# The last expert of each mixture of experts: its gated rows split and loaded ahead, its result in two column halves

## The chip, the cores and the metric
The kernel runs on one core of one Trainium2 chip. The metric is device time in microseconds (us), the median of three runs. One execution is also taken by the hardware profiler, and the trace is of that one. Engines are named as in the profile: PE is TensorE (matmul), PEld its weight loads, DVE is VectorE, ACT is ScalarE, POOL is GpSimd, SP is SyncE.

## The reference
Two layers of a diffusion backbone over 512 tokens of width 1024: layer 0 mixes with retention and differential attention, layer 1 with a pooling mixer. Each layer ends in a mixture of 16 experts with hidden width 512, of which each token uses two:

```
for e in range(N_EXPERTS):
    hid = silu(flat @ w_gate[e]) * (flat @ w_up[e])
    out = out + combine[:, e:e + 1] * (hid @ w_down[e])
x = x + g2 * out
```

The output is the RMS norm of x after both layers. Everything is fp32.

## The kernel before
The program is a row of stages, each a block with one instruction stream per engine, closed by a barrier of all engines. The stages that matter here are the two mixtures (`moe(0)` ahead of the pooling layer, `moe(1)` ahead of the final norm). After each of them a stage follows that does nothing unless an expert has more than 128 tokens, and then a stage whose first work is on POOL: eight indirect DMAs (L2165) that gather each token's two result rows from `y_dram` in HBM. Those rows are written by the mixture, so the mixture's stage ends only when its last store has landed.

A mixture works on one expert at a time, on at most 128 of its tokens. For fp32 accuracy each matmul operand is split into a high part (fp32r) and a low part (the rest), and each product is three matmuls: high by high, high rows by low weights, low rows by high weights. ACT makes the high parts (`high`, L1725, for the weights; L1732 for the rows; `hid_high`, L1741, for the gated rows), and DVE the low parts (`low`, L1879; L1886; `hid_low`, L1896). The weights of an expert come in six halves p = 0 to 5: gate (0, 1), up (2, 3) and down (4, 5), loaded by SP into a ring (L475). The parts of a half live in one of four buffers, `buf(u, p)`.

Step e holds the down product of expert e and the gate and up products of expert e + 1. On PE its order is: gate product of e + 1 (24 matmuls of 512 columns, L1978), four transposes of the gated rows of e (L2006) into PSUM bank 4, eight transposes for the rows of expert e + 2 (L1961), up product of e + 1 (24 matmuls), and the down product of e (`down`, L1993, 12 matmuls for each of p = 4 and 5) into banks 6 and 7. On DVE: low part of half 0, low part of the rows, the gating of e + 1 (`hidden`, L1892), low parts of halves 1 to 3, the result of expert e - 1 out of banks 6 and 7 times the layer's gate (`rows_out`, L1903), `hid_low`, and the low parts of halves 4 and 5. On ACT: the high parts in step with this, `hid_high`, the silu for e + 1, the store of e - 1 (L1745, a DMA on ACT's own queue) and the high part of half 5. All of this is in program order on each engine, with semaphores that count: `s_used` for halves that PE is done with, `s_hi` and `s_lo` for parts, `s_ht2`, `s_hhi` and `s_hlo` for the gated rows' transposes, high and low parts, `s_y` for results and `s_yst` for stores.

Step 15, the last, has no expert after it. It is only: transposes of the gated rows of 15, `hid_high`, `hid_low`, the parts of its two down halves, its 24 down matmuls, the eviction of all 1024 columns and one store of 512 KB.

Of the kernel before, what the change touches and what calls it, by code (L numbers as in the profile page):

```python
# [31 lines left out]
P = 128  # L32
# [7 lines left out]
HALF = 512  # L40
# [70 lines left out]
def build_program(nc, a, out):  # L111
    ctx = ExitStack()
    with ctx, nc.allow_non_contiguous_dma(reason="short rows of small tables"):
# [71 lines left out]
        def stage_sb(name, shape, dt=F32):  # L185
            return mem["stack"].enter_context(nc.sbuf_tensor(f"{name}{mem['stages']}", shape, dt))
# [1362 lines left out]
        def moe(l):  # L1549
# [17 lines left out]
            xT_lo = stage_sb("xT_lo", [P, KD, P], F32R)  # L1567
            hT_hi = stage_sb("hT_hi", [P, KE, P], F32R)
            hT_lo = stage_sb("hT_lo", [P, KE, P], F32R)

            mark = stage_sb("mark", [1, 1])

# [53 lines left out]
            def last_step(e):  # L1626
                return isinstance(e, int) and e == LAST

            def buf(u, p):

                return (2 * u + p) % 4
# [4 lines left out]
            def pos_count(e, p):  # L1636

                return count(6, p - 4 if last_step(e) else p, e)
# [11 lines left out]
            with nc.Block() as block:  # L1650
# [65 lines left out]
                @block.scalar  # L1716
                def _(act):
                    def high(e, u, p):

                        act.wait_ge(half_load[raw(e, p)], loaded(e, p))  # L1720
                        if isinstance(e, int) and e == 0 and p < 4:
                            act.wait_ge(s_used, (1, 2, 3, 6)[p])
                        elif not (isinstance(e, int) and e == -1):
                            act.wait_ge(s_used, pos_count(e, p) - 4)
                        nc.scalar.copy(w_hi[:, buf(u, p), :], half(raw(e, p))).then_inc(s_hi, 3 if isinstance(e, int) and (e, p) == (-1, 3) else 1)  # L1725

                    def rows_high(n, b, up_used):

                        act.wait_ge(s_gt, n + 1)
                        if up_used is not None:  # L1730
                            act.wait_ge(s_used, up_used)
                        nc.scalar.copy(xT_hi[:, b].rearrange("p k t -> p (k t)"),  # L1732
                                       bank[:, 0:2, :].rearrange("p b c -> p (b c)")).then_inc(s_xhi, 1)

                    def silu(n, gate_used):
                        act.wait_ge(s_used, gate_used)
                        nc.scalar.activation(act_g, bank[:, 2, :], ACT.Silu).then_inc(s_silu, 1)

                    def hid_high(n):
                        act.wait_ge(s_ht2, n + 1)  # L1740
                        nc.scalar.copy(hT_hi[:].rearrange("p k t -> p (k t)"), bank[:, 4, :]).then_inc(s_hhi, 1)  # L1741

                    def store(e, u):
                        act.wait_ge(s_y, e + 1)
                        act.dma_start(y_dram[bass.ds(e * P, P), :], y_sb[:, u, :]).then_inc(s_yst[u], 16)  # L1745

                    def step(e, u):
                        if isinstance(e, int) and e == 0:
                            high(0, 0, 0)
                            silu(0, pos_count(-1, 1))  # L1750
                            rows_high(1, 1, None)
                            for p in (1, 2, 3):
                                high(0, 0, p)
                        elif not last_step(e):
                            high(e, u, 0)
                            rows_high(e + 1, 1 - u, pos_count(e, 3) - 12)
                            for p in (1, 2, 3):
                                high(e, u, p)
                        high(e, u, 4)
                        hid_high(e)  # L1760
                        if not last_step(e):
                            act.wait_ge(s_hid, e + 1)
                            silu(e + 1, pos_count(e, 1))
                        if not (isinstance(e, int) and e == 0):
                            store(e - 1, 1 - u)
                        high(e, u, 5)

                    for p in range(4):
                        high(-1, 0, p)
                    rows_high(0, 0, None)  # L1770
                    step(0, 0)
                    with act.Fori(0, (NE - 4) // 2) as i:
                        for v in range(2):
                            step(2 * i + 1 + v, 1 - v)
                    for e in range(NE - 3, NE):
                        step(e, e % 2)
                    store(NE - 1, 1)
                    for u in range(2):
                        act.wait_ge(s_yst[u], 16 * (NE // 2 + 1))

                @block.vector
                def _(dve):
# [93 lines left out]
                    def low(e, u, p):  # L1876

                        dve.wait_ge(s_hi, pos_count(e, p))
                        V.tensor_tensor(w_lo[:, buf(u, p), :], half(raw(e, p)), w_hi[:, buf(u, p), :].bitcast(F32),  # L1879
                                        ALU.subtract).then_inc(s_lo, 3 if isinstance(e, int) and (e, p) == (-1, 3) else 1)  # L1880

                    def rows_low(n, b, up_used):
                        dve.wait_ge(s_xhi, n + 1)
                        if up_used is not None:
                            dve.wait_ge(s_used, up_used)
                        V.tensor_tensor(xT_lo[:].rearrange("p k t -> p (k t)"), bank[:, 0:2, :].rearrange("p b c -> p (b c)"),  # L1886
                                        xT_hi[:, b].rearrange("p k t -> p (k t)").bitcast(F32), ALU.subtract).then_inc(s_xlo, 1)
# [3 lines left out]
                        dve.wait_ge(s_silu, n + 1)  # L1891
                        V.tensor_tensor(hid, act_g, bank[:, 3, :], ALU.mult).then_inc(s_hid, 1)  # L1892

                    def hid_low(n):
                        dve.wait_ge(s_hhi, n + 1)
                        V.tensor_tensor(hT_lo[:].rearrange("p k t -> p (k t)"), bank[:, 4, :],  # L1896
                                        hT_hi[:].rearrange("p k t -> p (k t)").bitcast(F32), ALU.subtract).then_inc(s_hlo, 1)

                    def rows_out(n, u, down_used, stored):

# [3 lines left out]
                                        ALU.mult).then_inc(s_y, 1)  # L1904

                    def step(e, u, stored):
                        if not last_step(e):
                            low(e, u, 0)
                            rows_low(e + 1, 1 - u, pos_count(e, 3) - 6)
                        hidden(e, 6 * (e + 1) - 2)  # L1910
                        if not last_step(e):
                            low(e, u, 1)
                            low(e, u, 2)
                            low(e, u, 3)
                        if stored is not None:
                            rows_out(e - 1, 1 - u, 6 * (e + 1), stored)
                        hid_low(e)
                        low(e, u, 4)
                        low(e, u, 5)
# [8 lines left out]
                    with dve.Fori(0, (NE - 4) // 2) as i:  # L1928
                        for v in range(2):
                            step(2 * i + 1 + v, 1 - v, 16 * i + 16)  # L1930
                    for e in range(NE - 3, NE):
                        step(e, e % 2, 16 * ((e - 1) // 2) + 16)
                    rows_out(NE - 1, 1, pos_count(LAST, 5), 16 * (LAST // 2) + 16)

                @block.tensor
                def _(pe):
# [57 lines left out]
                                                     start=(kk == 0 and i == 0), stop=(kk == KE - 1 and i == 2))  # L1994
                        last.then_inc(s_used, 1)

                    def step(e, u, gathered):

                        if not last_step(e):
                            pe.wait_ge(s_xlo, e + 2)  # L2000
                            pe.wait_ge(s_silu, e + 1)
                            product(2, e, u, 0, 1 - u)
                            product(2, e, u, 1, 1 - u)
                        pe.wait_ge(s_hid, e + 1)
                        for k in range(KE):
                            last = pe.transpose(bank[:, 4, k * P:(k + 1) * P], hid[:, k * P:(k + 1) * P], ident[:])  # L2006
                        last.then_inc(s_ht2, 1)
                        if gathered is not None:
                            rows_T(u, gathered)
                        if not last_step(e):  # L2010
                            product(3, e, u, 2, 1 - u)
                            product(3, e, u, 3, 1 - u)
                        pe.wait_ge(s_hlo, e + 1)
                        if not (isinstance(e, int) and e == 0):
                            pe.wait_ge(s_y, e)
                        down(e, u, 4)
                        down(e, u, 5)

                    keep_busy(16)
                    rows_T(0, 16)  # L2020
# [8 lines left out]
                    with pe.Fori(0, (NE - 4) // 2) as i:  # L2029
                        for v in range(2):  # L2030
                            step(2 * i + 1 + v, 1 - v, 16 * i + 16 * (2 + v))
                    for e in range(NE - 3, NE):
                        step(e, e % 2, 16 * ((e + 2) // 2 + 1) if e + 2 < NE else None)

            stage_over()

# [363 lines left out]
```

## Time and profile before

| | us |
|---|---|
| median of three runs (1180.56 to 1181.78) | 1181.64 |
| the profiled execution | 1180.51 |
| its span in the profile | 1178.7 |
| PE busy | 1044.6 (89%) |
| DVE busy | 928.9 (79%) |
| ACT busy | 608.0 (52%) |
| POOL busy | 162.1 (14%) |

Times in the rows are in us from the start of the span. "Idle before" a group is how long its engine did nothing ahead of it, and "<-" names what ended that. A matmul row's length is that of the whole pass through the array, so neighbouring matmuls overlap: what one costs in a stream is the distance between two starts. PEclk is the share of full speed that was granted to TensorE's clock. The expert products of the first mixture run from 474 to 764, and those of the second end at 1147.

### The profile page before, as it was taken

What the parts mean: (1) busy time and instruction counts of PE and PEld (TensorE: products, weight loads), DVE (VectorE), ACT (ScalarE), POOL (GpSimd) and SP (SyncE); (2) the same over time, 40 slices, a digit from 0 to 9 for tenths busy, and PEclk for the clock granted to TensorE, in tenths of its full rate; (3) what the DMA queues carried; (4) which work ended last, traced back from release to release, by engine and by line L of the source; (5) the groups of instructions that cost most, each with busy time, mean ns of one, the idle gap of its engine ahead of it and who ended that gap; (6) DMA issues with size and microseconds to landing.
All of it is one profiled execution on the core that took longest, in us unless ns stands there. A gap on an engine that the chain in (4) does not pass through costs nothing. (4 is left out here: it accounts for less than half of the span.)

```text
span 1178.7 us, 13896 instructions
## 1 busy us (share of the span) xinstructions
PE 1044.6 (89%) x4832; PEld 795.7 (68%) x4832; DVE 928.9 (79%) x1041; ACT 608.0 (52%) x614; POOL 162.1 (14%) x172
## 2 busy tenths in 40 slices
PE   6789999998898987999999999738799999999970
PEld 1476767766565445788888888637578888888850
DVE  4578888877993336799999999555759999999955
ACT  1534222213664113677777777333367777777831
POOL 0100200000100002522212210041341000000006
PEclk9899999999999997999999999959799999999995
DMA  9715878676014003999999999576399999999936
GB/s 372 263 64 206 284 283 302 223 281 232 7 66 134 36 29 135 301 412 414 413 414 414 413 414 413 206 250 274 98 269 401 414 413 414 414 414 414 413 131 232
DMA packets 145693, 332.44 MB, mean 282 GB/s; under 512 B 14064, under 2 KB 16056, under 8 KB 145520
## 3 DMA queue, kind: packets, MB, share of 16 engines
q1 hardware_dynamic: 125768, 277.99, 62.3%
q10 hardware_dynamic: 12392, 28.68, 6.5%
q0 software_dynamic: 7488, 25.19, 5.7%
q8 instruction: 26, 0.43, 0.1%
q14 instruction: 19, 0.16, 0.0%
HBM read 308.72 MB, written 23.15 MB: 282 GB/s over the span
## 5 line engine op out<-in xcount | busy, mean ns | idle before, releaser
L1879 DVE TENSOR_TENSOR w_lo<-ring,w_hi 128x2048 fp32r<-128x2048 f32 x192 | 432.2, 2287 | 26.1 <-ACT w_hi L1725 22.5
L1725 ACT CAST w_hi<-ring 128x2048 fp32r<-128x2048 f32 x192 | 365.4, 1915 | 135.2 <-DMA ring<-in_moe_w_up 59.8
L1978 PE MATMUL bank<-w_hi,xT_hi 128*128 128x512 f32 x512 | 203.4, 397 | 6.7 <-DVE xT_lo L1886 5.2
L1978 PE MATMUL bank<-w_hi,xT_lo 128*128 128x512 f32 x512 | 199.9, 390 | 0.0
L1978 PE MATMUL bank<-w_lo,xT_hi 128*128 128x512 f32 x512 | 199.4, 389 | 0.0
L1399 PE MATMUL bank<-ring_last_parts,arena_parts 128*128 128x512 f32 (+1 forms) x320 | 117.1, 397 | 5.4 <-DVE ring_parts L1016 2.7
L1978 PEld LDWEIGHTS bank<-w_hi,xT_hi 128*128 128x128 f32 x512 | 96.1, 188 | 28.4 <-DVE xT_lo L1886 6.9
L1978 PEld LDWEIGHTS bank<-w_hi,xT_lo 128*128 128x128 f32 x512 | 96.1, 188 | 20.8
L1074 DVE SCALAR_TENSOR_TENSOR gate_b<-ring,silu_c,gate_b 128x512 f32<-128x512 f32 x140 | 105.9, 757 | 4.5
L1978 PEld LDWEIGHTS bank<-w_lo,xT_hi 128*128 128x128 f32 x512 | 96.3, 188 | 19.0
L1993 PE MATMUL bank<-w_hi,hT_hi 128*128 128x512 f32 x256 | 101.0, 394 | 7.5 <-DVE w_lo L1879 7.5
L1993 PE MATMUL bank<-w_lo,hT_hi 128*128 128x512 f32 x256 | 101.1, 395 | 0.0
L1993 PE MATMUL bank<-w_hi,hT_lo 128*128 128x512 f32 x256 | 100.9, 394 | 0.0
L1399 PE MATMUL bank<-ring_parts,arena_parts 128*128 128x512 f32 (+1 forms) x256 | 99.9, 390 | 0.0
L1399 PEld LDWEIGHTS bank<-ring_last_parts,arena_parts 128*128 128x128 f32 x320 | 60.1, 191 | 31.5 <-issue 13.2
L1399 PE MATMUL bank<-ring_last_parts,x_parts 128*128 128x512 f32 x192 | 76.8, 400 | 0.0
L1682 POOL DMA_INDIRECT shared<-xh_scratch,shared x32 | 62.6, 1957 | 60.7 <-DVE shared L1870 52.6
L1993 PEld LDWEIGHTS bank<-w_hi,hT_hi 128*128 128x128 f32 x256 | 48.9, 191 | 18.5 <-issue 8.3
L767 ACT CAST ring_last_parts<-ring 128x1024 fp32r<-128x1024 f32 x24 | 25.2, 1051 | 67.2 <-PE bank L1399 61.5
L1993 PEld LDWEIGHTS bank<-w_hi,hT_lo 128*128 128x128 f32 x256 | 48.9, 191 | 10.3
L1993 PEld LDWEIGHTS bank<-w_lo,hT_hi 128*128 128x128 f32 x256 | 48.6, 190 | 10.2
L1903 DVE TENSOR_TENSOR shared<-bank,gate_b 128x1024 f32<-128x1024 f32 x32 | 39.0, 1219 | 19.8 <-PE bank L1993 19.8
(254 smaller groups left out, 1397.5 us busy)
## 6 DMA issues: line engine op xcount, KB each, us to landing
ring<-in_moe_w_gate SPq DMA_DIRECT2D x64, 1024.0 KB
ring<-in_moe_w_up SPq DMA_DIRECT2D x64, 1024.0 KB, 13.4
ring<-in_moe_w_down SPq DMA_DIRECT2D x64, 1024.0 KB, 11.6
ring<-in_ada_w SPq DMA_DIRECT2D x21, 2048.0 KB, 8.6
y_scratch<-shared ACTq DMA_DIRECT2D x32, 512.0 KB, 6.1
ring<-in_w_in ACTq DMA_DIRECT2D x21, 512.0 KB, 3.8
shared<-in_ada_w SPq DMA_DIRECT2D x2, 2048.0 KB, 16.0
x_res<-in_x SPq DMA_DIRECT2D x8, 512.0 KB, 12.4
```

The source lines that it names most:

```text
L767: nc.scalar.copy(w_high(n), w_raw(n)).then_inc(m_whi, 1)
L1074: ins = nc.vector.scalar_tensor_tensor(ada_acc[:, i % 2, :], w[:, k, :], silu_c[:, 0, k:k + 1], onto, ALU.mult, ALU.add)
L1399: last = pe.matmul(acc(u)[:, c0:c1], hs[h_], ws[w_], start=(kk == 0 and i == 0), stop=(kk == KD - 1 and i == 2))
L1682: pool.indirect_dma_start(out=xg[:, u, :], out_offset=None, in_=xh_dram, in_offset=bass.IndirectOffsetOnAxis(ap=idx[:, c:c + 1], axis=0)). ...
L1725: nc.scalar.copy(w_hi[:, buf(u, p), :], half(raw(e, p))).then_inc(s_hi, 3 if isinstance(e, int) and (e, p) == (-1, 3) else 1)
L1879: V.tensor_tensor(w_lo[:, buf(u, p), :], half(raw(e, p)), w_hi[:, buf(u, p), :].bitcast(F32), ALU.subtract).then_inc(s_lo, 3 if isinstance ...
L1903: V.tensor_tensor(y_sb[:, u, :], bank[:, 6:8, :].rearrange("p b c -> p (b c)"), gate2_b[:], ALU.mult).then_inc(s_y, 1)
L1978: last = pe.matmul(bank[:, b, :], xs[:, kk, :], ws[:, k, :], start=(kk == 0 and i == 0), stop=(kk == KD - 1 and i == 2))
L1993: last = pe.matmul(bank[:, 6 + hf, :], xs[:, kk, :], ws[:, k, at], start=(kk == 0 and i == 0), stop=(kk == KE - 1 and i == 2))
```

## The change
In the step of expert 14, the four transposes of expert 15's gated rows are put between the two halves of expert 14's down product. The high and low parts of those gated rows go into new places, `hT_last_hi` and `hT_last_lo`, which are the two halves of a buffer for expert rows that is free by then. On ACT both high parts of expert 15's down halves now come ahead of `hid_high`, and the store of expert 14 comes after it. On DVE the order after step 14 is: gating of 15, low part of half 4, `hid_low`, low part of half 5, `rows_out` of expert 14, and then the result of 15 in two halves of 512 columns. On PE `down_last` takes the place of `down` for expert 15: it writes banks 0 and 1 and not 6 and 7, does all 12 matmuls of one column half (both p) and then all 12 of the other, and each is stored by a DMA of its own. The branches `last_step` in the helpers go.

```diff
+            hT_last_hi, hT_last_lo = xT_hi[:, 0, 0:KE, :], xT_hi[:, 0, KE:KD, :]
...
 act:
-                    for e in range(NE - 3, NE):
+                    for e in range(NE - 3, LAST):
                         step(e, e % 2)
-                    store(NE - 1, 1)
+                    high(LAST, 1, 4)
+                    high(LAST, 1, 5)
+                    hid_high(LAST, hT_last_hi)
+                    store(LAST - 1, 0)
+                    for hf in range(2):
+                        act.wait_ge(s_y, LAST + 1 + hf)
+                        cols_ = slice(hf * HALF, (hf + 1) * HALF)
+                        act.dma_start(y_dram[LAST * P:NE * P, cols_], y_sb[:, 1, cols_]).then_inc(s_yst[1], 16)
                     for u in range(2):
-                        act.wait_ge(s_yst[u], 16 * (NE // 2 + 1))
+                        act.wait_ge(s_yst[u], 16 * (NE // 2 + 1 + u))
...
 dve:
-                    for e in range(NE - 3, NE):
+                    for e in range(NE - 3, LAST):
                         step(e, e % 2, 16 * ((e - 1) // 2) + 16)
-                    rows_out(NE - 1, 1, pos_count(LAST, 5), 16 * (LAST // 2) + 16)
+                    hidden(LAST, 6 * NE - 2)
+                    low(LAST, 1, 4)
+                    hid_low(LAST, hT_last_hi, hT_last_lo)
+                    low(LAST, 1, 5)
+                    rows_out(LAST - 1, 0, 6 * NE, 16 * ((LAST - 1) // 2) + 16)
+                    dve.wait_ge(s_yst[1], 16 * (LAST // 2) + 16)
+                    for hf in range(2):
+                        dve.wait_ge(s_used, pos_count(LAST, 4 + hf))
+                        cols_ = slice(hf * HALF, (hf + 1) * HALF)
+                        V.tensor_tensor(y_sb[:, 1, cols_], bank[:, hf, :], gate2_b[:, cols_], ALU.mult).then_inc(s_y, 1)
...
 pe, in step(e, u, gathered):
                         down(e, u, 4)
+                        if isinstance(e, int) and e == LAST - 1:
+                            hid_T(LAST)
                         down(e, u, 5)
+                    def down_last():
+                        pe.wait_ge(s_hlo, NE)
+                        for hf in range(2):
+                            at = slice(hf * HALF, (hf + 1) * HALF)
+                            for p in (4, 5):
+                                parts(LAST, p)
...
+                                for k in range(KE // 2):
+                                    kk = (p % 2) * (KE // 2) + k
+                                    for i, (xs, ws) in enumerate(((hT_last_hi, hi), (hT_last_hi, lo), (hT_last_lo, hi))):
+                                        last = pe.matmul(bank[:, hf, :], xs[:, kk, :], ws[:, k, at],
+                                                         start=(kk == 0 and i == 0), stop=(kk == KE - 1 and i == 2))
+                            last.then_inc(s_used, 1)
```

## Rows read from the trace of the kernel before

**Rows 1.** The page: busy time, and granted clock in 40 slices.
```profile
PE 1044.6 (89%) x4832; PEld 795.7 (68%) x4832; DVE 928.9 (79%) x1041; ACT 608.0 (52%) x614; POOL 162.1 (14%) x172
PEclk9899999999999997999999999959799999999995
```
**Rows 2.** Waits from 1120 to 1178: engine line <- releaser: total us, times, longest.
```profile
DVE shared L1903 <- PE bank L1993: 9.9, 2, 5.3
PE bank L1993 <- DVE w_lo L1879: 3.8, 1, 3.8
```
**Rows 3.** Timeline of PE, second mixture's end: start, length, engine, line, names.
```profile
1122.36 0.60 PE L2006 MATMUL bank<-ident,shared 128*128 128x128 f32 x4
...
1125.57 0.39 PE L1978 MATMUL bank<-w_hi,xT_hi 128*128 128x512 f32 x1
...
1128.29 0.39 PE L1993 MATMUL bank<-w_hi,hT_hi 128*128 128x512 f32 x1
...
1131.01 0.39 PE L1993 MATMUL bank<-w_hi,hT_hi 128*128 128x512 f32 x1
...
1133.73 0.60 PE L2006 MATMUL bank<-ident,shared 128*128 128x128 f32 x4
1138.10 0.47 PE L1993 MATMUL bank<-w_hi,hT_hi 128*128 128x512 f32 x1 [3.77 <-DVE w_lo L1879]
...
1139.54 0.63 PE L1993 MATMUL bank<-w_hi,hT_lo 128*128 128x512 f32 x1
1139.97 0.63 PE L1993 MATMUL bank<-w_hi,hT_hi 128*128 128x512 f32 x1
...
1145.00 0.39 PE L1993 MATMUL bank<-w_hi,hT_lo 128*128 128x512 f32 x1
```
**Rows 4.** Timeline of DVE, the same stretch.
```profile
1123.61 0.69 DVE L1896 TENSOR_TENSOR hT_lo<-bank,hT_hi 128x512 fp32r<-128x512 f32 x1 [0.66 <-ACT hT_hi L1741]
...
1128.62 0.68 DVE L1892 TENSOR_TENSOR shared<-shared,bank 128x512 f32<-128x512 f32 x1
1133.93 1.23 DVE L1903 TENSOR_TENSOR shared<-bank,gate_b 128x1024 f32<-128x1024 f32 x1 [4.63 <-PE bank L1993]
...
1135.67 4.48 DVE L1879 TENSOR_TENSOR w_lo<-ring,w_hi 128x2048 fp32r<-128x2048 f32 x2
...
1145.43 1.23 DVE L1903 TENSOR_TENSOR shared<-bank,gate_b 128x1024 f32<-128x1024 f32 x1 [5.28 <-PE bank L1993]
```
**Rows 5.** Timeline of ACT, the same stretch.
```profile
1122.99 0.59 ACT L1741 CAST hT_hi<-bank 128x512 fp32r<-128x512 f32 x1 [1.07 <-PE bank L2006]
...
1123.97 3.77 ACT L1725 CAST w_hi<-ring 128x2048 fp32r<-128x2048 f32 x2
1134.36 0.59 ACT L1741 CAST hT_hi<-bank 128x512 fp32r<-128x512 f32 x1 [6.63 <-PE bank L2006]
...
1146.68 0.34 ACTq L1745 DMA_DIRECT2D y_scratch<-shared  x1
```
**Rows 6.** DMA from 1146 to 1153: GB/s in 40 slices of 0.175 us; issues.
```profile
GB/s 0 0 0 0 0 0 0 0 164 421 421 421 421 374 445 328 0 0 0 0 0 0 0 0 0 0 0 0 0 0 0 0 0 0 0 0 0 0 70 140
...
y_scratch<-shared ACTq DMA_DIRECT2D x1, 512.0 KB, 2.6
```
**Rows 7.** Stretches: length, PE, PEld, DVE, ACT, POOL, clock, DMA share, GB/s.
```profile
1128.00:1128.50 0.50, 0.50 (x3) 0.40 (x3) 0.50 (x1) 0.00 (x0) 0.00 (x0) 1.00 0.04 16
1128.50:1129.00 0.50, 0.50 (x4) 0.41 (x3) 0.50 (x2) 0.00 (x0) 0.00 (x0) 1.00 0.00 0
1138.10:1145.40 7.30, 7.29 (x24) 5.54 (x24) 2.05 (x1) 0.00 (x0) 0.00 (x0) 0.77 0.01 2
```
**Rows 8.** Timelines of PE, DVE, POOL and SP, first mixture's end.
```profile
752.10 0.58 SPq L1676 DMA_DIRECT2D mod<-k_band_sum  x1
...
756.55 0.58 PE L1993 MATMUL bank<-w_hi,hT_hi 128*128 128x512 f32 x1 [3.77 <-DVE w_lo L1879]
...
763.89 1.23 DVE L1903 TENSOR_TENSOR shared<-bank,gate_b 128x1024 f32<-128x1024 f32 x1 [5.29 <-PE bank L1993]
...
771.66 0.94 POOL L2165 DMA_INDIRECT arena<-y_scratch,row_of  x1 [78.93 <-issue]
```
**Rows 9.** Timeline of POOL after the second mixture.
```profile
1153.02 0.94 POOL L2165 DMA_INDIRECT shared<-y_scratch,row_of  x1 [80.77 <-issue]
```

More of the change, by code:

```diff
@@ L1737, in silu, with hid_high @@
                         nc.scalar.activation(act_g, bank[:, 2, :], ACT.Silu).then_inc(s_silu, 1)
-                    def hid_high(n):
+                    def hid_high(n, into=hT_hi[:]):
                         act.wait_ge(s_ht2, n + 1)
-                        nc.scalar.copy(hT_hi[:].rearrange("p k t -> p (k t)"), bank[:, 4, :]).then_inc(s_hhi, 1)
+                        nc.scalar.copy(into.rearrange("p k t -> p (k t)"), bank[:, 4, :]).then_inc(s_hhi, 1)
                     def store(e, u):
@@ L1753, in step @@
                                 high(0, 0, p)
-                        elif not last_step(e):
+                        else:
                             high(e, u, 0)
@@ L1760, in step @@
                         hid_high(e)
-                        if not last_step(e):
-                            act.wait_ge(s_hid, e + 1)
-                            silu(e + 1, pos_count(e, 1))
+                        act.wait_ge(s_hid, e + 1)
+                        silu(e + 1, pos_count(e, 1))
                         if not (isinstance(e, int) and e == 0):
@@ L1892, in hidden, with hid_low @@
                         V.tensor_tensor(hid, act_g, bank[:, 3, :], ALU.mult).then_inc(s_hid, 1)
-                    def hid_low(n):
+                    def hid_low(n, hi=hT_hi[:], into=hT_lo[:]):
                         dve.wait_ge(s_hhi, n + 1)
-                        V.tensor_tensor(hT_lo[:].rearrange("p k t -> p (k t)"), bank[:, 4, :],
-                                        hT_hi[:].rearrange("p k t -> p (k t)").bitcast(F32), ALU.subtract).then_inc(s_hlo, 1)
+                        V.tensor_tensor(into.rearrange("p k t -> p (k t)"), bank[:, 4, :],
+                                        hi.rearrange("p k t -> p (k t)").bitcast(F32), ALU.subtract).then_inc(s_hlo, 1)
                     def rows_out(n, u, down_used, stored):
@@ L1906, in step @@
                     def step(e, u, stored):
-                        if not last_step(e):
-                            low(e, u, 0)
-                            rows_low(e + 1, 1 - u, pos_count(e, 3) - 6)
+                        low(e, u, 0)
+                        rows_low(e + 1, 1 - u, pos_count(e, 3) - 6)
                         hidden(e, 6 * (e + 1) - 2)
[L1911 to L1914, printed above, removed]
+                        low(e, u, 1)
+                        low(e, u, 2)
+                        low(e, u, 3)
                         if stored is not None:
@@ L1995, in down, with hid_T @@
                         last.then_inc(s_used, 1)
[L1997 to L2003, printed above, removed]
+                    def hid_T(e):
                         pe.wait_ge(s_hid, e + 1)
@@ L2007, in step @@
                         last.then_inc(s_ht2, 1)
+                    def step(e, u, gathered):
+                        pe.wait_ge(s_xlo, e + 2)
+                        pe.wait_ge(s_silu, e + 1)
+                        product(2, e, u, 0, 1 - u)
+                        product(2, e, u, 1, 1 - u)
+                        hid_T(e)
                         if gathered is not None:
                             rows_T(u, gathered)
-                        if not last_step(e):
-                            product(3, e, u, 2, 1 - u)
-                            product(3, e, u, 3, 1 - u)
+                        product(3, e, u, 2, 1 - u)
+                        product(3, e, u, 3, 1 - u)
                         pe.wait_ge(s_hlo, e + 1)
@@ L2016, in step @@
                         down(e, u, 4)
+                        if isinstance(e, int) and e == LAST - 1:
+                            hid_T(LAST)
                         down(e, u, 5)
+                    def down_last():
[4 more added lines that the diff above has]
+                                parts(LAST, p)
+                                hi = w_hi[:, buf(1, p), :].rearrange("p (k c) -> p k c", c=D)
+                                lo = w_lo[:, buf(1, p), :].rearrange("p (k c) -> p k c", c=D)
+                                for k in range(KE // 2):
[4 more added lines that the diff above has]
+                            last.then_inc(s_used, 1)
                     keep_busy(16)
@@ L2031, in _ @@
                             step(2 * i + 1 + v, 1 - v, 16 * i + 16 * (2 + v))
-                    for e in range(NE - 3, NE):
+                    for e in range(NE - 3, LAST):
                         step(e, e % 2, 16 * ((e + 2) // 2 + 1) if e + 2 < NE else None)
+                    down_last()
             stage_over()
```

## The prediction
> **What bounds the kernel now.** The page comes first. PE is busy 89% of the span and its clock is nearly full in almost every slice [rows 1], so inside the mixtures' steady steps PE sets the pace, and the change leaves those steps alone. The chain of waits reaches back only to the barrier behind the second mixture, so for the mixture's end I go to the waits of the last 60 us: two entries stand out, DVE waiting for PE's down products and PE waiting 3.8 us for a low part [rows 2]. The timelines place them. The up product of expert 15 ends and the down product of 14 runs from 1128.29 to 1133.73 without a hole. Then come the four transposes, and PE does nothing until the down product of 15 starts at 1138.10 [rows 3]. This end is a single file: transposes, high part on ACT at 1134.36 [rows 5], low part on DVE, the low part of half 4 from 1135.67 [rows 4], 24 matmuls, an eviction of 1.23 us, a store issued at 1146.68 [rows 5], its landing, and the barriers before POOL's first gather at 1153.02 [rows 9]. DVE, which makes the part that PE waits for, had itself waited 4.63 us before that for PE [rows 4]. The first mixture has the same end, about 381.5 us earlier: PE starts at 756.55 behind the same hole of 3.77 us, and the last eviction starts at 763.89 [rows 8]. Nothing follows either mixture that could have started without its last store, so what the file loses in length the kernel loses in time, twice.
>
> **The change part by part** (times of the second mixture).
>
> *Transposes moved.* The first half of the down product of 14 ends, by starts, at 1131.01 (12 matmuls in 2.72 us, 0.2267 each) [rows 3]. The transposes need the gating of 15, which runs from 1128.62 to 1129.30 [rows 4], so PE finds it done 1.7 us before. The cost of four transposes within a stream is read at 1122.36: from there to the matmul at 1125.57, which is the thirteenth after them, 3.21 us pass where 12 matmuls take 2.72 [rows 3]. So they cost 0.49 us, and the second half of the down product of 14 ends at 1131.01 + 3.21 = 1134.22.
>
> *What stands behind on ACT.* After step 14 ACT now makes both high parts of 15. The row of two casts from 1123.97 to 1127.74 already holds half 5 of expert 14 and half 4 of 15 [rows 5]; nothing moves there. The cast of half 5 of 15 was behind `hid_high` and ran at 1135.6. It needs its buffer, which PE frees with the last up matmul, about 1128.5, and its weights. The stretches show the DMA traffic of the load end before 1128.5 [rows 7]. So it runs 1128.5 to 1130.4, and ACT is free 1.2 us before `hid_high`, which follows the transposes by 0.63 us as at 1122.99 [rows 3, 5]: 1131.64.
>
> *What stands behind on DVE.* The low part of half 4 follows the gating, 1129.2 to 1131.5 (2.29 us; two take 4.48 [rows 4]). `hid_low` follows `hid_high` by 0.62, as 1123.61 follows 1122.99 [rows 4, 5]: 1132.26. The low part of half 5 begins 0.61 later, 1132.87, and ends at 1135.16. Then `rows_out` of 14 from about 1135.1 to 1136.3, whose banks are complete since 1134.4. Its store is issued at 1136.3, a microsecond later than now, and lands long before the end.
>
> *The down product of 15.* PE waits for `hid_low` (done at 1132.95) and half 4 (1131.5), so it begins at once at 1134.22 and not at 1138.10: **3.88 us** earlier. Because the column half is now the outer loop, half 5 is needed at the seventh matmul and not at the thirteenth: 1134.22 + 6 x 0.2267 = 1135.58. With the 0.14 us that PE took after the low part of half 4 ended at 1137.96 [rows 3, 4], half 5 is there at 1135.30. The cover is 0.28 us: thin, and worth its excess if it fails.
>
> *The clock.* Now the clock falls about a microsecond after PE takes up work behind its 3.77 us of rest: starts are 0.43 us apart at 1139.54, the granted clock of the stretch is 0.77 [rows 3, 7], which is a part at 1.2 and a part at 2.4 GHz. The last matmul starts 6.90 us after the first; at full clock it is 23 x 0.2267 = 5.21. If the hole goes, so should the fall: **1.69 us**. Bounds: nothing if the clock falls anyway, 1.69 if it doesn't. I take all of it, because the step's earlier transposes at 1122.36 sit in a stream whose pitch stays 0.23 [rows 3].
>
> *The eviction.* The last matmul starts at 1134.22 + 5.21 = 1139.43. The new banks leave PE no wait for `rows_out` of 14. The first column half is complete at about 1137.1 and evicted beside PE's second half. DVE took up the last result 0.43 us after the last start (1145.00, 1145.43), so the second half begins at 1139.86. A gating of 512 columns out of PSUM takes 0.68 us [rows 4], against 1.23: **0.55 us**. The issue follows at 1140.55 instead of 1146.68. So far 3.88 + 1.69 + 0.55 = 6.12 (rounded starts make it 6.13).
>
> *The store.* 512 KB takes 2.6 us from issue to landing, of which data flows for 8 slices of 0.175 us, 1.4 us, at some 420 GB/s [rows 6]. The last one is now 256 KB with pieces of 2 KB: 0.7 us less at that rate, nothing less if small pieces or the wait for the write eat it. The store of the first half goes out at 1137.8 and is through by then. I take **0.6 us**, nearer to the transfer's share. The Trainium skill (DMA: Bandwidth & Descriptors, section Anatomy of one DMA) gives an estimate of 2.0 us plus the bytes at 436 GB/s, which would be 3.2 us for the old store and 2.6 for the new. The row has 2.6 for the old one, so the fixed part is smaller here than the page's. If its 2.6 for the new one held all the same, this term would be nothing and the kernel 1.2 us longer than I say.
>
> *Behind it.* From the eviction's start to POOL's first gather are 7.77 us in the first mixture and 7.59 in the second [rows 4, 8, 9]; the barriers in that are unchanged. In the first mixture SP also loads tables for the next stage; its last issue is at 752.10 [rows 8], and the last store there is now issued at 1140.55 - 381.5 = 759.0.
>
> **Sum.** 6.1 + 0.6 = 6.7 us for each mixture, 13.4 for both. The profiled execution took 1180.51 (span 1178.7 and 1.8 around it): 1167.1. The median of the runs lies 1.1 above the profiled one: **1168.2**.
>
> **The rivals.**
> *A wait inside the new file (late half 5).* The cover at the seventh matmul is 0.28 us, and the load of half 5 lands only shortly before its cast. For it: the second mixture's loads run close to their use (the DMA is still busy at 1128 [rows 7]). Against it: ACT has 1.2 us to spare. If the cast or `hid_low` comes 1 to 2 us late, PE stands that long in each mixture: 2 to 4 us in all, 1171.
> *The clock falls anyway,* with some matmuls of the last expert slow. The price is the 1.69 us kept, twice: 1171.6. Against it is the stream around 1122.36.
> *The gain is hidden at the stage's end.* If another engine or SP's tables held the barrier, one mixture would give little: 1168.2 + 6.7 = 1174.9. The tables' rows speak against it, and for the second mixture I see nothing that runs so late.
> *Slower.* The transposes now stand in front of 12 matmuls of expert 14 as well as of the 24 of 15. If the clock fell there and stayed down until the end, 36 matmuls would start 0.43 and not 0.227 apart, 36 x 0.20 = 7.2 us more than in the sum, against its gain of 6.7. That is 0.5 us worse than now in each mixture, 1182.6, and more if the fall begins in the first half of that product too (12 x 0.20 = 2.4 us a mixture: 1187.4). It decides from the 34th slow matmul, 6.7 by 0.20. The transposes at 1122.36 caused no such fall, and now it ends by itself after some 8 slow starts (1.69 by 0.20).
>
> **How the numbers follow.** The forecast has 0.76, with an own range of 1166.0 to 1169.6; the late half 0.10; the clock 0.06; the hidden end 0.05; slower 0.03. The lower end, 1166.0, is the forecast less the 1.2 us by which the three runs spread and 0.5 us in each mixture, 0.1 from the store and 0.4 from releases that I took from single rows. The upper end of its own range has the store saving nothing (1.2) and 0.2; the full range also takes in the late half and the clock: 1166.0 to 1172.0. About 0.2% (2.4 us) is what a measurement can tell from no change: faster 0.96, same 0.02, slower 0.02.
>
> **What would show it.** In the profile after: the four transposes at 1131 (less the first mixture's gain) between two groups of down matmuls; no wait of PE for a low part near the end, or one of under a few tenths of a microsecond; 24 starts 0.227 apart with a granted clock of 1.00; two evictions of 0.68 us, the second 0.43 us behind the last start; two stores of 256 KB, the last landing in about 2 us; the first gathers 6.7 and 13.4 us earlier. It is wrong if PE's hole is still there under another name, if starts 0.43 us apart appear after the transposes, or if the gathers come no earlier than now.

## The result, and the profile after

The changed kernel's median is 1167.12 us (1164.08 to 1170.69, 5 runs); runs of the kernel before, interleaved with it and added to the first three, give 1180.56 (1175.93 to 1181.78, 5 runs). The ratio is 0.990, 95% interval 0.9881 to 0.9919: faster by 9.6 to 14.0 us. In a later repeat the ratio was 0.989 (0.9871 to 0.9908), 1164.83 against 1178.99. Forecast were 1168.2, a range of 1166.0 to 1172.0, and 13.4 us less.

The profiled execution took 1164.08 us (span 1162.2). The page first, busy time and granted clock in 40 slices, to be held against [rows 1]:

```profile
PE 1037.1 (89%) x4832; PEld 790.4 (68%) x4832; DVE 928.3 (80%) x1043; ACT 608.6 (52%) x614; POOL 140.4 (12%) x172
PEclk9899999998999998999999999969899999999995
```

The same number of matmuls now keeps PE busy 7.5 us less. Some 3 us of that is the last experts' down products at full clock: PE was busy 7.25 and 7.29 us in them and is busy 5.77 and 5.68. What the rest is was not followed. POOL's fall to 140.4 is spread: it is between 139.4 and 181.8 in the profiles of all kernels here. The timeline of PE at the second mixture's end is the answer to [rows 3] (start, length, engine, line, names; a row of two is two matmuls merged):

```profile
1113.11 0.60 PE L2014 MATMUL bank<-ident,shared 128*128 128x128 f32 x4
...
1119.04 0.39 PE L2007 MATMUL bank<-w_hi,hT_hi 128*128 128x512 f32 x1
...
1121.76 0.60 PE L2014 MATMUL bank<-ident,shared 128*128 128x128 f32 x4
1122.11 0.49 PE L2007 MATMUL bank<-w_hi,hT_hi 128*128 128x512 f32 x1
...
1124.98 0.39 PE L2047 MATMUL bank<-w_hi,xT_hi 128*128 128x512 f32 x1
...
1130.19 0.39 PE L2047 MATMUL bank<-w_hi,xT_hi 128*128 128x512 f32 x1
```

The second group of four transposes stands between two groups of down matmuls of expert 14 (L2007), and the last expert's down product (L2047) follows at 1124.98 with no idle time shown anywhere. Its 24 starts span 5.21 us, where [rows 3] had 6.90.

DVE in the same stretch, for [rows 4]:

```profile
1119.37 0.68 DVE L1899 TENSOR_TENSOR shared<-shared,bank 128x512 f32<-128x512 f32 x1
1119.97 2.28 DVE L1886 TENSOR_TENSOR w_lo<-ring,w_hi 128x2048 fp32r<-128x2048 f32 x1
1123.01 0.69 DVE L1903 TENSOR_TENSOR xT_hi<-bank,xT_hi 128x512 fp32r<-128x512 f32 x1 [0.76 <-ACT xT_hi L1742]
1123.62 2.28 DVE L1886 TENSOR_TENSOR w_lo<-ring,w_hi 128x2048 fp32r<-128x2048 f32 x1
1125.82 1.22 DVE L1910 TENSOR_TENSOR shared<-bank,gate_b 128x1024 f32<-128x1024 f32 x1
1127.97 0.69 DVE L1947 TENSOR_TENSOR shared<-bank,gate_b 128x512 f32<-128x512 f32 x1 [0.93 <-PE bank L2047]
1130.62 0.69 DVE L1947 TENSOR_TENSOR shared<-bank,gate_b 128x512 f32<-128x512 f32 x1 [1.96 <-PE bank L2047]
```

The reader should see that the gated rows' low part (1123.01) stands between the two low parts of the weights, and that the last result leaves in two pieces of 0.69 us, the first beside PE's second column half. The high part and the stores on ACT (the last row is two stores merged; the second is issued at 1131.34):

```profile
1122.39 0.59 ACT L1742 CAST xT_hi<-bank 128x512 fp32r<-128x512 f32 x1 [1.19 <-PE bank L2014]
1127.07 0.34 ACTq L1746 DMA_DIRECT2D y_scratch<-shared  x1
1128.69 2.99 ACTq L1784 DMA_DIRECT2D y_scratch<-shared  x2
```

The DMA issues of this stretch (times each, KB each, us to landing), for [rows 6], the busy times of the last product (length, PE, PEld, DVE, ACT, POOL, clock, DMA share, GB/s), for [rows 7], and POOL's first gather, for [rows 9]:

```profile
y_scratch<-shared ACTq DMA_DIRECT2D x1, 512.0 KB, 2.6
y_scratch<-shared ACTq DMA_DIRECT2D x2, 256.0 KB, 2.0
```
```profile
1124.90:1130.70 5.80, 5.68 (x26) 4.36 (x24) 2.91 (x4) 0.00 (x0) 0.00 (x0) 1.00 0.35 138
```
```profile
1137.04 0.94 POOL L2198 DMA_INDIRECT shared<-y_scratch,row_of  x1 [74.05 <-issue]
```

The first mixture, for [rows 8], does the same:

```profile
747.65 0.60 PE L2014 MATMUL bank<-ident,shared 128*128 128x128 f32 x4
...
756.51 0.69 DVE L1947 TENSOR_TENSOR shared<-bank,gate_b 128x512 f32<-128x512 f32 x1 [1.96 <-PE bank L2047]
...
763.13 0.94 POOL L2198 DMA_INDIRECT arena<-y_scratch,row_of  x1 [74.24 <-issue]
```

**Where the time came from.** The spans differ by 16.5 us, more than the change accounts for, so it is measured where it acts: from the four transposes in the step of expert 14 to POOL's first gather, "the stretch" from here on. In the second mixture it was 1153.02 - 1122.36 = 30.66 us and is 1137.04 - 1113.11 = 23.93, 6.73 less. In the first the step's transposes start at 740.81 before and 739.00 after: 771.66 - 740.81 = 30.85 and 763.13 - 739.00 = 24.13, 6.72 less. Together that is 13.45. The other 3.1 us lie outside: 1.8 ahead of the first stretch, 0.7 between the two and 0.5 behind.

### The profile page after: what moved, and what is told of

Read it like the earlier page. It is cut to its first block and busy times, and to the rows that moved or that the text cites. A ratio compares the mean times of both kernels' runs of the same rounds, so it can differ in the third digit from the quotient of the medians.

```text
span 1162.2 us, 13900 instructions
## 1 busy us (share of the span) xinstructions
PE 1037.1 (89%) x4832; PEld 790.4 (68%) x4832; DVE 928.3 (80%) x1043; ACT 608.6 (52%) x614; POOL 140.4 (12%) x172
## 5 line engine op out<-in xcount | busy, mean ns | idle before, releaser
L2007 PE MATMUL bank<-w_hi,hT_hi 128*128 128x512 f32 x240 | 93.7, 390 | 0.0
L2007 PE MATMUL bank<-w_lo,hT_hi 128*128 128x512 f32 x240 | 93.4, 389 | 0.0
L2007 PE MATMUL bank<-w_hi,hT_lo 128*128 128x512 f32 x240 | 93.4, 389 | 0.0
L1399 PEld LDWEIGHTS bank<-ring_parts,arena_parts 128*128 128x128 f32 x256 | 48.5, 189 | 8.6
L2007 PEld LDWEIGHTS bank<-w_hi,hT_hi 128*128 128x128 f32 x240 | 45.1, 188 | 9.6 <-issue 0.3
L2007 PEld LDWEIGHTS bank<-w_hi,hT_lo 128*128 128x128 f32 x240 | 45.0, 188 | 9.4
L2007 PEld LDWEIGHTS bank<-w_lo,hT_hi 128*128 128x128 f32 x240 | 45.0, 188 | 9.2
L1713 POOL CAST shared<-shared 128x1 uint32<-128x1 int32 x26 | 7.5, 288 | 347.5 <-PE bank L1975 337.5
## 6 DMA issues: line engine op xcount, KB each, us to landing
ring<-in_moe_w_up SPq DMA_DIRECT2D x64, 1024.0 KB, 13.4
```

What stands on the lines that cost most here:

```text
L1399: last = pe.matmul(acc(u)[:, c0:c1], hs[h_], ws[w_], start=(kk == 0 and i == 0), stop=(kk == KD - 1 and i == 2))
L1713: nc.gpsimd.tensor_copy(idx[:, u:u + 1], lists[:, m:m + 1]).then_inc(s_idx, 1)
L2007: last = pe.matmul(bank[:, 6 + hf, :], xs[:, kk, :], ws[:, k, at], start=(kk == 0 and i == 0), stop=(kk == KE - 1 and i == 2))
```

## The experiments

In the table, "last start" is the distance on PE from the transposes of expert 15's gated rows to the last matmul (first mixture, second mixture). Each ratio is against runs of the kernel before on the same chip at the same time, with medians of 1178.29 (e1 to e4), 1177.51 (e5 to e8) and 1178.99 us (e9, e10); a time without a ratio is a single run.

| kernel | stretch, us | last start, us | time, us | ratio (95%) |
|---|---|---|---|---|
| before | 30.85, 30.66 | 11.29, 11.27 | 1180.56 | |
| changed | 24.13, 23.93 | 8.43, 8.43 | 1167.12 | 0.990 (0.9881 to 0.9919) |
| e1 transposes late | 26.64, 26.46 | 8.22, 8.23 | 1171.28 | 0.9937 (0.9916 to 0.9958) |
| e2 whole result | 25.35, 25.16 | 8.43, 8.43 | 1166.29 | 0.9895 (0.9859 to 0.993) |
| e3 old banks | 26.44, 28.02 | 10.71, 12.32 | 1171.44 | 0.9931 (0.9903 to 0.9958) |
| e4 hole filled | 29.30, 29.06 | 9.69, 9.70 | 1176.55 | 0.9975 (0.996 to 0.9991) |
| e5 halves alone | 29.74, 29.53 | 11.30, 11.30 | 1176.92 | |
| e6 cover cut | 25.05, 24.82 | 9.32, 9.32 | 1167.24 | |
| e7 one store | 24.73, 24.64 | 8.43, 8.43 | 1163.64 | |
| e8 three pieces | 24.07, 23.57 | 8.69, 8.69 | 1165.12 | 0.9875 (0.9838 to 0.9912) |
| e9 changed again | 24.14, 23.95 | 8.43, 8.43 | 1164.83 | 0.989 (0.9871 to 0.9908) |
| e10 old banks again | 26.41, 26.39 | 10.69, 10.68 | 1169.96 | |

In e1 the transposes themselves stand 2.7 us later in the step, so its last start is to be read with that added; the same holds for before, e4 and e5. The totals that were expected for e1 (1172.5 to 1176) and e2 (1169.4) came out lower, 1171.28 and 1166.29; the stretches came out within 0.3 us of what was expected, e8's apart.

**e1: the transposes late again**

```diff
                         down(e, u, 4)
-                        if isinstance(e, int) and e == LAST - 1:
-                            hid_T(LAST)
                         down(e, u, 5)
+                        if isinstance(e, int) and e == LAST - 1:
+                            hid_T(LAST)
```

> The changed kernel with one part undone: the four transposes of expert 15's gated rows stand behind both halves of expert 14's down product again. Measure: the stretch from the four transposes of step 14 to POOL's first gather (24.13 us in the first mixture and 23.93 in the second of the changed kernel, 30.85 and 30.66 before). Theory (single file, the hoist fills PE's hole): high part, low part and the low part of half 5 now follow transposes at about 1134.0 on the old time base, so half 5 is there at 1138.3 and PE's last matmul starts 2.7 us later: about 26.7 us in each mixture, up to 28.4 if the clock falls in the new hole of some 2 us; 1172.5 to 1176 in all. Rival (the gain comes from making parts of half 4 and 5 ahead, the place of the transposes hardly matters): at most 0.5 us more, 24.6.

The stretch is 2.5 us longer in both mixtures, and 2.5 us of that is PE's. PE waits twice, and the waits are named in the timeline of PE of this kernel:

```profile
1130.70 0.50 PE L2047 MATMUL bank<-w_hi,xT_hi 128*128 128x512 f32 x1 [1.40 <-DVE xT_hi L1903]
1132.90 0.50 PE L2047 MATMUL bank<-w_hi,xT_hi 128*128 128x512 f32 x1 [0.54 <-DVE w_lo L1886]
```

First for the gated rows' low part, then at the seventh matmul for half 5. The granted clock stayed at 1.00 through both. The rival, that the place of the transposes hardly matters, is out: the hoist makes 2.5 of the 6.7 us, and the rest of the change keeps 4.2 (30.85 - 26.64). Of these 4.2 the column halves are 1.1 (e5) and the clock some 1.6 (e4), so an estimate of 1.5 is left for making the parts earlier; no run has that alone.

**e2: the result whole, and e7: one store behind two evictions**

```diff
 e2, pe
-                        for hf in range(2):
...
-                            for p in (4, 5):
...
+                        for p in (4, 5):
...
+                            for hf in range(2):
...
 e2, dve
-                    for hf in range(2):
...
-                        V.tensor_tensor(y_sb[:, 1, cols_], bank[:, hf, :], gate2_b[:, cols_], ALU.mult).then_inc(s_y, 1)
...
+                    V.tensor_tensor(y_sb[:, 1, :], bank[:, 0:2, :].rearrange("p b c -> p (b c)"), gate2_b[:],
+                                    ALU.mult).then_inc(s_y, 1)
 e2 and e7, act
-                    for hf in range(2):
...
-                        act.dma_start(y_dram[LAST * P:NE * P, cols_], y_sb[:, 1, cols_]).then_inc(s_yst[1], 16)
...
+                    act.dma_start(y_dram[LAST * P:NE * P, :], y_sb[:, 1, :]).then_inc(s_yst[1], 16)
...
```

> The changed kernel with its column halves undone: down product with p as the outer loop as before, still in banks 0 and 1, one eviction of 1024 columns and one store of 512 KB. Theory: the eviction costs 0.55 us more and the store 0.6, so the stretch is 25.1 us in each mixture (24.0 now), 1169.4 in all; PE's stream stays whole, at full clock. Rival (the inner order matters, because half 5 is needed later in this order, or 2 KB pieces cost the store time): the stretch stays under 24.5.

> The changed kernel with its two evictions, but one store of 512 KB behind both. Theory: only the transfer's share comes back, 0.6 us: stretch 24.6 us in each mixture, landing 2.6 us where the half store has 2.0. Rival (small pieces make the half store as slow, the gain was in the eviction): 24.0.

e2 is longer by 1.22 and 1.23 us, and PE's part did not change by a hundredth. e7 is longer by 0.60 and 0.71, the transfer's share; in both kernels the last store of 512 KB lands in 2.6 us again. What is left between e2 and e7, 0.62 and 0.52, is the eviction of 512 columns instead of 1024. The totals show none of this: e2's median of 4 runs is below the changed kernel's, because runs of one kernel spread by 5 us and more (5.5 in e2's own four) and this is 2.4.

**e3 and e10: the old banks**

```diff
 dve
-                        V.tensor_tensor(y_sb[:, 1, cols_], bank[:, hf, :], gate2_b[:, cols_], ALU.mult).then_inc(s_y, 1)
+                        V.tensor_tensor(y_sb[:, 1, cols_], bank[:, 6 + hf, :], gate2_b[:, cols_], ALU.mult).then_inc(s_y, 1)
 pe
+                        pe.wait_ge(s_y, LAST)
...
-                                        last = pe.matmul(bank[:, hf, :], xs[:, kk, :], ws[:, k, at],
+                                        last = pe.matmul(bank[:, 6 + hf, :], xs[:, kk, :], ws[:, k, at],
```

> The changed kernel, but the last result goes to banks 6 and 7 as before, so that PE has to wait for the eviction of expert 14's result, which DVE makes behind the low part of half 5. Theory: PE waits until 1.22 us after that low part ends, 2.2 us in each mixture: stretch 26.2 us, up to 27.9 if the clock falls behind that hole; 1171.5 to 1175 in all. Rival (own banks save nothing, as before the change PE never waited for that eviction): 24.0 us.

> The changed kernel with banks 6 and 7 once more. In its first profile PE's hole of 2.00 us was followed by a full clock in the first mixture (stretch 26.44 us) and by slow starts in the second (28.02 us). Theory (a hole of this length may or may not bring the clock down): each mixture shows one of these two, 26.4 or 28.0. Rival (something of the second mixture alone brings the clock down): again 26.4 in the first and 28.0 in the second.

PE now waits 2.00 us ahead of the last product in all four cases (two kernels, two mixtures). The profile names no releaser for this wait, but the edit and the times do: in e3's second mixture the eviction of expert 14's result runs from 1129.83 to 1131.05, and PE starts at 1131.14. The stretch of three of them is 26.4 us, 2.3 to 2.5 more than with own banks. The fourth is 28.0, and the stretches of the two last products in e3 say why (length, PE, PEld, DVE, ACT, POOL, clock, DMA share, GB/s), first and second mixture:

```profile
755.00:762.00 7.00, 5.72 (x24) 4.43 (x24) 1.52 (x3) 0.00 (x0) 0.00 (x0) 1.00 0.30 115
1131.10:1138.50 7.40, 7.33 (x24) 5.59 (x24) 0.69 (x1) 0.00 (x0) 0.00 (x0) 0.77 0.26 106
```

The same hole brought the clock down once and not the three other times. Since e10 had it full in the second mixture, it isn't something of that mixture. So the own banks are a necessary part of this order, though before the change no wait of PE for them shows.

**e4: the hole filled in the kernel before**

```diff
+                        if last_step(e):
+                            for _ in range(14):
+                                pe.matmul(bank[:, 0, :], xT_hi[:, 0, 0, :], xT_hi[:, 0, 0:KE, :], start=True, stop=True)
                         pe.wait_ge(s_hlo, e + 1)
```

> The kernel before, with 14 matmuls of 512 columns that nobody reads put into PE's hole behind the last transposes (14 x 0.227 = 3.2 us of the 3.77). The first down matmul of expert 15 should start where it did. Theory (the clock fell because of the hole): starts 0.227 apart throughout, granted clock 1.00, and the stretch is 1.69 us shorter in each mixture: 29.0 to 29.2 us where it was 30.7 to 30.9; 1177.2 in all. Rival (the clock falls there for another reason, and the change's gain has another source): the starts are 0.43 apart for some 8 matmuls as before, and the stretch stays 30.7.

The timeline of PE: the fillers, and then the down product of 15.

```profile
1132.09 0.60 PE L2006 MATMUL bank<-ident,shared 128*128 128x128 f32 x4
1132.44 3.48 PE L2015 MATMUL bank<-xT_hi 128*128 128x512 f32 x14
1136.45 0.47 PE L1993 MATMUL bank<-w_hi,hT_hi 128*128 128x512 f32 x1 [0.53 <-DVE w_lo L1879]
...
1141.79 0.39 PE L1993 MATMUL bank<-w_hi,hT_lo 128*128 128x512 f32 x1
```

It starts 4.36 us after the transposes (4.37 before), and its starts span 5.34 us where they spanned 6.90. Nothing moved except the clock. The stretch is 1.55 and 1.60 us shorter and the whole kernel 0.25% (0.1% to 0.4%). The clock's fall belonged to the hole.

**e5: the column halves alone, on the kernel before**

```diff
-                        down(e, u, 4)
-                        down(e, u, 5)
+                        if last_step(e):
+                            for hf in range(2):
+                                for p in (4, 5):
+                                    ...
+                                last.then_inc(s_used, 1)
+                        else:
+                            down(e, u, 4)
+                            down(e, u, 5)
```

> The kernel before with the column halves alone: the last down product in banks 6 and 7, column half as the outer loop, two evictions of 512 columns, two stores; transposes, casts and low parts where they were. Theory: the end gains 0.55 (eviction) and 0.6 (store), but half 5, ready at 1140.3, is now needed at the seventh matmul, 1138.1 + 1.36 = 1139.5, so PE stands 0.8 us, some of which replaces slow clocked starts: stretch 29.7 to 30.4 us in each mixture, before 30.7 and 30.9. Rival (the halves are the main part of the gain): 26 us or less.

The stretch is 1.11 and 1.13 us shorter, eviction and store. (The fence shows PE's part; the two evictions and two stores are made as in the change.) The stand of 0.8 us for half 5 that I expected did not come. PE's timeline shows the reason:

```profile
1135.63 0.47 PE L2033 MATMUL bank<-w_hi,hT_hi 128*128 128x512 f32 x1 [3.77 <-DVE w_lo L1882]
...
1137.46 0.63 PE L2033 MATMUL bank<-w_hi,hT_lo 128*128 128x512 f32 x1
1137.89 0.65 PE L2033 MATMUL bank<-w_hi,hT_hi 128*128 128x512 f32 x1
1138.34 0.63 PE L2033 MATMUL bank<-w_lo,hT_hi 128*128 128x512 f32 x1
```

The clock had fallen, so the seventh matmul came 2.26 us after the first and not 1.36; the low part of half 5 was done (1133.21 + 4.48 = 1137.69) 0.2 us ahead of it.

**e6: the cover taken away**

```diff
                     hid_low(LAST, hT_last_hi, hT_last_lo)
+                    V.tensor_tensor(xT_lo[:].rearrange("p k t -> p (k t)"), gate2_b[:], gate2_b[:], ALU.mult)
                     low(LAST, 1, 5)
```

> The changed kernel with one more DVE instruction of 1024 columns (about 1.14 us from start to start, its result unread) between the low part of the gated rows and the low part of half 5. Theory: the cover at the seventh matmul of the last product is 0.3 us, so PE stands 1.14 - 0.3 = 0.84 us there in each mixture: stretch 24.8 us and 24.9, clock still full. Rival (the cover is larger, because PE is held by something else at the end): nothing changes, 24.0.

The stretch is 0.92 and 0.89 us longer, and PE names the wait at its seventh matmul:

```profile
1127.18 0.39 PE L2048 MATMUL bank<-w_hi,xT_hi 128*128 128x512 f32 x1
...
1129.29 0.50 PE L2048 MATMUL bank<-w_hi,xT_hi 128*128 128x512 f32 x1 [0.59 <-DVE w_lo L1886]
1129.63 0.40 PE L2048 MATMUL bank<-w_lo,xT_hi 128*128 128x512 f32 x1
```

The instruction took 1.13 us of DVE (1125.82 to 1126.95). The seventh matmul starts 2.11 us after the first and not 1.36, so it is 0.75 us late, and the cover was 1.13 - 0.75 = 0.38 us. The other 0.14 us of the 0.89 come behind the wait, from starts that are a little further apart (0.34 us for the first, 0.227 in a steady stream). The idle time in the row, 0.59, is shorter than the delay because a matmul row is longer than the distance between starts.

**e8: three pieces**

```diff
-                        for hf in range(2):
-                            at = slice(hf * HALF, (hf + 1) * HALF)
+                        for hf, (c0, c1) in enumerate(((0, 512), (512, 768), (768, 1024))):
+                            at = slice(c0, c1)
```

> The changed kernel with the last result in pieces of 512, 256 and 256 columns, three evictions and three stores. The last eviction and the last store get smaller (about 0.3 us each by the step from 1024 to 512 columns), but PE has 24 matmuls of 256 columns where it had 12 of 512. Theory A (weight loads, 0.188 us each in the rows, set the pace of short matmuls): 24 x 0.19 = 4.5 us for 2.7, 1.8 us more, less 0.6: stretch 25.2 us, slower than the changed kernel. Theory B (the pace follows the columns, 0.113 us): 0.6 us less: 23.4 us, better than both kernels.

(The loop changes in the same way in the streams of ACT and DVE.) Neither number came out, but theory B's reason nearly did. In the timeline of PE the last 24 matmuls are 0.12 us apart, and not the 0.19 of theory A:

```profile
760.03 0.40 PE L2047 MATMUL bank<-w_hi,xT_hi 128*128 128x256 f32 x2
760.27 0.28 PE L2047 MATMUL bank<-w_lo,xT_hi 128*128 128x256 f32 x1
760.39 0.40 PE L2047 MATMUL bank<-w_hi,xT_hi 128*128 128x256 f32 x2
```

24 of them cost 0.16 us more than 12 of 512 columns, and the last start comes 0.26 us later. The last eviction takes 0.42 us (0.69), the last store of 128 KB lands in 1.8 (2.0). The stretch is 0.06 us shorter in one mixture and 0.36 in the other; in the first, 0.3 us more pass behind the last store, and no run shows why. This is the shortest of all kernels here, but 0.4 us in 1165 can't be told by the totals; its ratio's interval contains the changed kernel's.

**e9: the changed kernel again**

> The changed kernel once more, without an edit, to see how exactly the stretch from the four transposes of step 14 to POOL's first gather comes back (24.13 and 23.93 us in its first profile) and where the runs' spread of some 5 us sits. Theory (the change is worth 6.7 us in each mixture and the rest of the first profile's 16.5 us is spread of other stages): the same stretch within 0.1 us, and a total that differs by what the stages ahead of it differ. Rival (part of the extra 3 us belongs to the change): the steps ahead of the first mixture's end are again 1.8 us earlier than in the kernel before (739.0 and not 740.8).

The stretch comes back within 0.02 us. The time ahead of it does not: the first matmul of the first mixture's experts starts at 474.1 us before, at 472.3 and 472.6 in the two profiles of the changed kernel, and at 478.4 in e8, whose code is the same up to there (counts, length in ns, first and last start; before, changed, e8):

```profile
L1978 PE MATMUL bank<-w_hi,xT_hi x512: 389/389/504, 474.1 to 1127.6; 128*128 128x512 f32 x171
```
```profile
L1992 PE MATMUL bank<-w_hi,xT_hi x512: 389/389/500, 472.3 to 1118.4; 128*128 128x512 f32 x171
```
```profile
L1992 PE MATMUL bank<-w_hi,xT_hi x512: 389/389/504, 478.4 to 1123.8; 128*128 128x512 f32 x171
```

From there to the step's transposes it is 266.7 us in all three profiles of before and changed, and 266.8 in e8. So the mixture's steps are alike, and the spread sits in the stages ahead and between. The 739.3 of e9 is what the rival named, and e2 and e7 have 739.0 and 739.4; but e1, e3, e6 and e10, with the same code up to this point, have 741.0 to 741.3, and e8 has 745.2. So the same code gives either start, and the 1.8 us can't be booked to the change. Why these stages differ from run to run was not tried.

## Why the prediction was right

- **The bound.** It was named as a single file at each mixture's end with nothing beside it; the two stretches shrank by 6.72 and 6.73 us where 6.7 was summed, and the stages behind took over all of it.
- **The transposes moved.** Predicted from the step's transposes at 1122.36: the hoisted group 8.65 us later, the last product 11.86 later. Measured: 8.65 and 11.87. But the prediction books all 3.88 us under the transposes. With the transposes late again (e1) PE's last start is only 2.5 us later. The other 1.4 us (from the step's transposes to the last start are 22.64 us before and 19.59 in e1; less 1.69 for the clock) go with the new order on ACT and DVE: half 4's parts are made ahead of the gated rows and the eviction of expert 14's result behind them. The prediction describes this order but gives it no price of its own.
- **ACT and DVE behind it.** The high part came 9.28 us after that mark (predicted 9.28), the gated rows' low part 9.90 (9.90), the end of the low part of half 5 12.79 (12.80). The cover at the seventh matmul, predicted at 0.28, was 0.38 by e6: the prediction allowed 0.14 us from the end of the low part to PE's start, and in e6 it was 0.06 (1129.23 to 1129.29).
- **The clock.** 1.69 us were counted for it. The last product's starts span 5.21 us and not 6.90, which is that; e4 isolates 1.56 (6.90 less 5.34), the rest being the slower starts behind the hole of 0.53 us that e4 leaves. That no hole is left is not needed for it: in e1 the clock stayed at 1.00 behind holes of 1.40 and 0.54 us.
- **Eviction and store.** 0.55 and 0.6 were counted. e2 and e7 give 0.52 to 0.62 and 0.60 to 0.71. The bound of 0.7 for the store was half of the 1.4 us of flow; at the rows' 421 GB/s, 256 KB are 0.62. The half store landed in 2.0 us. The Trainium skill's estimate (DMA: Bandwidth & Descriptors, section Anatomy of one DMA), 2.6 us for this size, is 0.6 too long here, as it was for the full store; its difference between the sizes, 0.6, agrees with the rows. That section gives its estimate for DMAs issued by way of GpSimd, which the prediction did not say, and this store is on ACT's queue.
- **The rivals.** The late half did not occur, but e6 shows how near it was. The clock did not fall in either profile of the changed kernel, nor in e2, e7 and e8, where PE's stream was as whole. Nothing else held the stage's end. Slower: the hoisted transposes left the pitch at 0.23.
- **The new wait that own banks avoid** was named only as "no wait"; e3 shows that it would have cost 2.3 to 2.5 us, and 4.1 when the clock fell.
- **What was off** is the spread. The first three runs lay within 1.2 us, and I took that for the noise. Over 17 runs made together the kernel before went from 1174.79 to 1182.47. The median came out 1.1 us from the forecast, inside that spread; the profiled execution itself was 1164.08 where 1167.1 was summed, and the median lay 3.0 above it where 1.1 was added. So the agreement of the total is partly luck; that of the stretches is not.

## What to carry to other kernels

At the end of a pipelined loop look for the single file: work of the last item that waits for the stage to drain, though its inputs were ready a step earlier. Sum the gain along that file from distances between starts, count with it the clock that a hole in PE costs afterwards, and check that the reordered work does not meet a buffer that the old order freed just in time. When runs spread by more than an edit is worth, measure the edit between two events in the profile on either side of it.

## What the runs showed of the hardware that I had not expected

- PE at rest for 2.00 us was followed by the lower clock (mean 0.77 in the product that followed) once in four; at rest for 3.77 us it was in both mixtures of before and in both of e5; with holes of 1.40 and 0.54 us (e1), 0.59 (e6) or 0.53 (e4) it stayed at 1.00.
- Matmuls of 256 columns ran 0.12 us apart, while each weight load's row is 0.19 us long. The length of a weight load's row is no lower bound on the distance between short matmuls.
- A store of 512, 256 and 128 KB landed in 2.6, 2.0 and 1.8 us. The last step saves 0.2, less than the 0.31 that 128 KB take at the 421 GB/s of [rows 6].
